# Rotation tables of a state-space layer: made later, on GpSimd, in the buffers where the scan reads them; weight chunks cut as halves; table work and loads in a new order

## The reference

```python
x = x + even_mixer(rms_norm(x, ...))          # RWKV-7 beside RG-LRU
x = x + conv_ffn(rms_norm(x, ...))            # first feed-forward
x = x + odd_mixer(rms_norm(x, ...))           # S5
x = x + conv_ffn(rms_norm(x, ...))            # second feed-forward
return rms_norm(x, final_norm_g)

def conv_ffn(xn, w_up, conv_w, conv_b, w_down):        # d_ff = 2816
    h = causal_dwconv(xn @ w_up, conv_w, conv_b)
    gate, val = split(h, 2)
    return (silu(gate) * val) @ w_down

def odd_mixer(xn, w_in, A_re, A_im, log_dt, B, C, D, w_glu):
    u = xn @ w_in                             # 64 groups of 16 channels, 64 complex states each
    ab = exp((A_re + i A_im) * dt); bb = (ab - 1) / A * B
    state[t] = ab * state[t-1] + bb @ u[t]    # associative scan over the sequence
    y = gelu(Re(C @ state) + D * u)
    val, gate = split(y @ w_glu, 2)
    return val * sigmoid(gate)
```

## Time and profile before

| | us |
|---|---|
| median of 3 runs (2630.66 to 2636.36) | 2632.98 |
| profiled execution, time | 2632.07 |
| its span | 2630.3 |

### The profile page before, as it was taken

The page is one execution under the profiler, slowest core; times in us unless marked ns, Lnnn a source line. Parts: engine busy times, 40 slices in busy tenths (PEclk is TensorE's granted clock), DMA queues, the critical chain, the costliest instruction groups (busy, mean ns, idle before and its releaser), DMA issues.

```text
span 2630.3 us, 33735 instructions
## 1 busy us (share of the span) xinstructions
PE 2481.5 (94%) x12861; PEld 2064.8 (78%) x12861; DVE 1473.8 (56%) x1902; ACT 1107.8 (42%) x1782; POOL 1320.7 (50%) x1120
## 2 busy tenths in 40 slices
PE   8999899999999999999888889999999999999997
PEld 6788788888777877887676668987878888888886
DVE  5442578786666676566656344663365656563223
ACT  5443345453445444453243334433254545452222
POOL 5322444453257767772577671112267777772221
PEclk9999999999999999999899889999999999999998
DMA  3111000000112222226344324651112222242312
GB/s 104 49 48 49 17 1 1 1 1 10 53 45 80 81 73 80 89 88 166 105 142 173 118 92 142 208 153 48 52 48 85 80 89 80 88 154 83 110 51 84
DMA packets 252963, 211.87 MB, mean 81 GB/s; under 512 B 25446, under 2 KB 228744, under 8 KB 250760
## 3 DMA queue, kind: packets, MB, share of 16 engines
q1 hardware_dynamic: 238599, 188.02, 22.8%
q10 hardware_dynamic: 14208, 21.76, 2.3%
HBM read 153.11 MB, written 52.43 MB: 78 GB/s over the span
## 4 chain that ended last, share of the span: by engine, by line
PE 59%; DVE 6%; POOL 5%; issue 2%; ACT 2%; DMA 0%; ACTq 0%; SPq 0%; DVEq 0%; POOLq 0%
PE acc_o L2172 14%; PE acc_o L1715 9%; PE bank_a L2172 8%; PE bank_a L2256 7%; PE bank_b L2256 7%; PE bank_b L2172 6%; PE acc_o L2713 2%; PE bank_a L3526 1%; POOL dense_lo L197 1%; PE bank_b L3549 1%; POOL t_gx L3051 1%; DVE x_late_l L2070 1%; POOL t_rot L3075 0%; DVE t_hx L3107 0%; POOL t_tmp L3075 0%
## 5 line engine op out<-in xcount | busy, mean ns | idle before, releaser
L197 POOL TENSOR_TENSOR dense_lo<-dense_raw,dense_hi 128x512 fp32r<-128x512 f32 (+3 forms) x142 | 178.2, 1256 | 494.4 <-ACT dense_hi L190 492.6
L190 ACT CAST dense_hi<-dense_raw 128x512 fp32r<-128x512 f32 (+3 forms) x142 | 79.4, 564 | 401.7 <-PE acc_o L1715 150.9
L2110 POOL TENSOR_TENSOR dense_lo<-w_raw_l,dense_hi 128x512 fp32r<-128x512 f32 x88 | 118.3, 1344 | 65.2 <-ACT dense_hi L2106 65.1
L2110 POOL TENSOR_TENSOR dense_lo<-w_sums_l,dense_hi 128x512 fp32r<-128x512 f32 x66 | 104.1, 1577 | 71.7 <-ACT dense_hi L2106 71.7
L2256 PE MATMUL bank_b<-h_hi_l,dense_hi 128*128 128x512 f32 x352 | 112.7, 402 | 26.0 <-POOL dense_lo L197 25.9
L403 PE MATMUL main_ps<-rounded 128*128 128x256 f32 x896 | 128.0, 294 | 8.9 <-DVE rounded L298 8.9
L197 POOL TENSOR_TENSOR w_lo_e<-w_raw_e,w_hi_e 128x512 fp32r<-128x512 f32 x42 | 56.3, 1344 | 158.0 <-ACT w_hi_e L190 158.0
L2110 POOL TENSOR_TENSOR w_l<-w_raw_l,w_l 128x512 fp32r<-128x512 f32 x88 | 115.0, 1306 | 40.9 <-ACT w_l L2106 40.9
L403 PEld LDWEIGHTS main_ps<-rounded 128*128 128x128 f32 x896 | 113.5, 190 | 27.3 <-DVE rounded L298 23.2
L2256 PE MATMUL bank_a<-h_hi_l,dense_hi 128*128 128x512 f32 x336 | 108.5, 405 | 23.7 <-POOL dense_lo L197 22.2
L2110 POOL TENSOR_TENSOR w_l<-w_sums_l,w_l 128x512 fp32r<-128x512 f32 x66 | 103.1, 1562 | 45.0 <-ACT w_l L2106 45.0
(11 more groups left out here) (544 smaller groups left out, 7085.7 us busy)
## 6 DMA issues: line engine op xcount, KB each, us to landing
w_raw_l<-in_f_w_up SPq DMA_DIRECT2D x176, 256.0 KB, 3.0
hidden<-val SPq DMA_DIRECT2D x44, 512.0 KB, 2.6
h_f_l<-hidden SPq DMA_DIRECT2D x44, 512.0 KB, 4.7
dense_raw<-in_f_w_down SPq DMA_DIRECT2D x72, 256.0 KB, 3.0
w_raw_e<-in_e_w_in SPq DMA_DIRECT2D x42, 256.0 KB, 2.9
s_states<-t_hx ACTq DMA_DIRECT2D x16, 512.0 KB, 2.9
s_inputs<-t_in ACTq DMA_DIRECT2D x16, 512.0 KB, 2.8
g_in<-s_inputs SPq DMA_DIRECT2D x8, 1024.0 KB, 5.2
```

The source lines that it names most:

```text
L190: nc.scalar.copy(self.hi[:, par, 0:n, :], self.raw[:, par, 0:n, :]).then_inc(w_hi_done, 1)
L197: pool.tensor_tensor(self.lo[:, par, 0:n, :], self.raw[:, par, 0:n, :], self.hi[:, par, 0:n, :].bitcast(F32), op=ALU.subtract).then_inc(w_ ...
L2110: pool.tensor_tensor(self.ring_lo[n % 4], self.source(ORDER[n % SEVEN]), self.ring_hi[n % 4].bitcast(F32), op=ALU.subtract).then_inc(q_lo, 1)
```

## The change

1. `chunks` cuts a unit in two nearly equal parts: 5 tiles as 3 and 2, 6 as 3 and 3; 7 and 8 stay 4 and 3, 4 and 4.
2. Rotation tables are made for four pairs at once, 8 times (`turns_pool(i, part)`), straight into `rot`, which has two buffers. Only table 0 is made in the first feed-forward (group 3, after the second chunk of units 2 and 3); table 1 at units 0 and 1 of the S5 product, tables 2 to 7 further on in it, each in two parts behind a chunk's subtraction. Table i waits for scan i-2. The stores and reads of `s5_turns` go, with their waits. `scan_dve` waits for POOL's count instead of a DMA.
3. A half on POOL is parted: products between the chunks, sums behind the second chunk.
4. `setup_dve(4)` moves to pair 11; steps 5, 6, 3 and 7 to units 1, 2, 3 and 7 of group 0; the transposes of C to units 3 and 5.
5. SP: B and C are loaded after the weights of unit 2 of group 0 instead of before them, hidden tiles of group 1 later; both first chunks of groups 1 to 3 ahead of the fetched tiles.
6. `first_act` makes `d_diag` first and stores the states last.

```diff
         def chunks(kt):
-            return [(k, min(KC, kt - k)) for k in range(0, kt, KC)]
+            n = (kt + 1) // 2
+            return [(0, n), (n, kt - n)]
...
             self.load_chunk(sp, 0, 1)
-            if self.tables:
-                self.tables.load_first_sp(sp, self.q_used0 + SEVEN * NP)
             for g in range(len(self.groups)):
                 fetched = list(self.next_tiles(g))
-                if g == 0:
-                    for m in fetched[:4]:
-                        self.fetch_sp(sp, m)
-                    self.hidden_sp(sp, NP - 1)
-                    fetched = fetched[4:]
-                else:
+                if g:
                     self.load_chunk(sp, g, 0)
-                    if self.tables:
-                        self.tables.beside_sp(sp, g, 1)
+                    self.load_chunk(sp, g, 1)
                     for m in fetched[:3]:
                         self.fetch_sp(sp, m)
-                    self.load_chunk(sp, g, 1)
                     fetched = fetched[3:]
                 for c in range(2, DT):
                     self.load_down(sp, g, c)
+                    if (g, c) == (0, 2):
+                        self.hidden_sp(sp, NP - 1)
+                        if self.tables:
+                            self.tables.load_first_sp(sp, self.q_used0 + SEVEN * NP)
                     for m in fetched[:2]:
                         self.fetch_sp(sp, m)
...
                     if self.tables:
-                        self.tables.beside_pool(pool, g, c)
+                        self.tables.beside_first_pool(pool, g, c)
                     if c > 1:
                         self.dn.take_lo(pool, n, self.down_unit(g) + c, 0, 1, 2)
+                    if self.tables:
+                        self.tables.beside_pool(pool, g, c, 2 * (self.down_unit(g) + c) + 4)
...
-    t_rot = [at(f"t_rot{s}", [P, 2, 2, N5], where) for s, where in enumerate((X_AT, Z_AT))]
+    rot = [at(f"rot{s}", [P, 4, 2, N5], where) for s, where in enumerate((Z_AT, Z_AT + 2 * TILE))]
+    t_tmp = at("t_tmp", [P, 2, 4, N5], X_AT + TILE)
...
             elif i in (8, 9, 10):
                 self.setup_dve(dve, i - 8)
+            elif i == 11:
+                self.setup_dve(dve, 4)
...
+        def beside_pool(self, pool, g, c, lo_done):
+            if self.half_of(g, c) is not None:
+                self.half_sums_pool(pool, self.half_of(g, c), lo_done)
+            elif g > self.HALF_GROUPS[-1] and c in (2, 3):
+                self.turns_pool(pool, 0, c - 2)
...
-        def turns_pool(self, pool, n):
-            pr = slice(2 * n, 2 * n + 2)
-            step = [P, 2, 8, 16]
+        def turns_pool(self, pool, i, part):
+            pr = slice(4 * i, 4 * i + 4)
+            step = [P, 4, 8, 16]
...
+            if part == 0:
+                if i == 0:
+                    pool.wait_ge(t_pe, 4 * HALVES)
+                    pool.wait_ge(t_kept, 11 * HALVES)
+                    pool.wait_ge(t_filters_out, 32 * HALVES)
+                elif i > 1:
+                    pool.wait_ge(s5_dve, 15 * (i - 1))
+                for o, a, b in ((turn[0], cos, far_cos), (tmp[0], sin, far_sin), (turn[1], sin, far_cos)):
+                    pool.tensor_tensor(o, a, b, op=ALU.mult).then_inc(t_turned, 1)
+            else:
+                pool.tensor_tensor(tmp[1], cos, far_sin, op=ALU.mult).then_inc(t_turned, 1)
+                pool.wait_ge(t_turned, 6 * i + 4)
+                pool.tensor_tensor(turn[0], turn[0], tmp[0], op=ALU.subtract).then_inc(t_turned, 1)
+                pool.tensor_tensor(turn[1], turn[1], tmp[1], op=ALU.add).then_inc(t_turned, 1)
...
-                read_turns(0)
                 load_unit(2)
                 read_filters(0)
                 read_states(0)
-                read_turns(1)
...
                 for n in range(DT):
-                    dn.take_lo(pool, DT, u_in + n, 0)
+                    for chunk in range(2):
+                        dn.take_lo(pool, DT, u_in + n, 0, chunk, chunk + 1)
+                        if n == 1:
+                            tables.turns_pool(pool, 1, chunk)
+                        elif n > 2:
+                            tables.turns_pool(pool, n - 1, chunk)
                 for n in range(len(PLACES)):
                     lo_place(pool, n)
+                    if n < 2:
+                        tables.turns_pool(pool, DT - 1, n)
...
-                    dve.wait_ge(rot_read[i % 2], 16 * (i // 2 + 1))
+                    dve.wait_ge(t_turned, 6 * i + 6)
```

More of the change, by code:

```diff
@@ L2216, in products_pe @@
                 down = self.down_unit(g)
-                for pair, k, n in self.pair_chunks(g):
+                for chunk, (pair, k, n) in enumerate(self.pair_chunks(g)):
                     for s in range(2):
@@ L2223, in products_pe @@
                             pe.wait_ge(f_lo, self.made + first + k + t + 2)
-                            last = self.down_tile(pe, g, s, k + t, self.down_place(g, k // KC, s), t)
+                            last = self.down_tile(pe, g, s, k + t, self.down_place(g, chunk, s), t)
                         last.then_inc(w_used, 1)
                     if self.tables:
-                        self.tables.beside_pe(pe, g, k // KC)
+                        self.tables.beside_pe(pe, g, chunk)
                 for c in range(2, DT):
@@ L2332, in load_sp @@
                     fetched = fetched[2:]
-                    if self.tables:
-                        self.tables.beside_sp(sp, g, c)
+                    if (g, c) == (0, 5) and self.tables:
+                        self.tables.load_second_sp(sp)
         def chunk_lo(self, pool, g, j):
@@ L3077, in turns_pool @@
[L3077 to L3084 removed]
+            if part == 0:
[12 more added lines that the diff above has]
+                pool.tensor_tensor(turn[1], turn[1], tmp[1], op=ALU.add).then_inc(t_turned, 1)
+                pool.wait_ge(t_turned, 6 * i + 6)
@@ L3138, in first_act @@
         def first_act(self, act, n):
-            self.keep_states(act, n)
+            for q in range(2):
+                nc.scalar.activation(d_diag[:, q, :], eye32[:, :], ACT.Copy,
+                                     scale=d_rows[:, 2 * n + q:2 * n + q + 1]).then_inc(t_kept, 1)
             act.wait_ge(t_pool, 8 * n + 8)
@@ L3143, in first_act @@
                                t_gx[:, part, :, 0, :].unsqueeze(2).to_broadcast([P, 2, 4, 32])).then_inc(t_kept, 1)
-            for q in range(2):
-                nc.scalar.activation(d_diag[:, q, :], eye32[:, :], ACT.Copy,
-                                     scale=d_rows[:, 2 * n + q:2 * n + q + 1]).then_inc(t_kept, 1)
+            self.keep_states(act, n)
         def half_act(self, act, n):
@@ L3186, in trunk @@
     fir = at("fir", [P, 4, 2, P], W_AT + 4 * TILE)
-    rot = at("rot", [P, 2, 4, 2, N5], W_AT + 5 * TILE)
     u_now = at("u_now", [P, 2, 4, 2, N5], B_AT)
@@ L3194, in trunk @@
     in_read, hx_read, fir_read = (sem(n + "_read") for n in ("in", "hx", "fir"))
-    rot_read = [sem(f"rot_read{s}") for s in range(2)]
     u_scaled = sem("u_scaled")
@@ L3396, in _ @@
                 ffn0.load_sp(sp)
-                for n in tables.TURNS[3, 7]:
-                    tables.keep_turns_sp(sp, n)
                 def load_unit(n):
@@ L3736, in up @@
                         ins.then_inc(s5_dve, 1)
-                    c_i, s_i = (rot[:, i % 2, :, k, :] for k in range(2))
+                    c_i, s_i = (rot[i % 2][:, :, k, :] for k in range(2))
                     up(nc.vector.tensor_copy(keep8[:, :, 1:N5], decay8[:, 4 * i:4 * i + 4].unsqueeze(2).to_broadcast([P, 4, N5 - 1])))
                     dve.wait_ge(s5_pe, inputs_done(i))
-                    dve.wait_ge(rot_read[i % 2], 16 * (i // 2 + 1))
+                    dve.wait_ge(t_turned, 6 * i + 6)
                     if i == DT - 1:
```

73 lines of the change are left out of this document (24 added, 49 removed).

## The result

The changed kernel takes 2570.69 us, the median of 4 runs (2568.31 to 2572.59), the kernel before 2632.36, also of 4. The ratio is 0.9763, its 95% interval 0.9746 to 0.978: 62 us faster. The forecast was 2564 us, the range 2546 to 2598. The profiled execution took 2569.76 us, its span is 2566.3, its mean clock 0.991.

What follows compares the result with a forecast made beforehand. PE, busy 94% of the span, was taken as the bound, its longest waits being for POOL's `dense_lo`. -66.5 - 2.4 - 1.5 + 1.2 = -69 from 2632.1 gave 2563, by the median 2564 us; range 2546 to 2598.

Steps and rivals of the forecast that it cites:

- The down part: First down product to first S5 product: 308 us instead of 374.5, 66 us less.
- Chunks of 3 and 2, sums behind: Down part: 2.7 us of PE work left after the first chunk's matmuls instead of 1.4; waits behind tables go.
- Group starts: Down part, two group starts: waits for the clearing of `t_fir` and ACT's copies, 4 us left, between 0 and 9.
- Loads in group 0: Unit 3's weights come late behind B and C in SP's queue: 5 us left, between 0 and 10.
- Table 0 in group 3: Its two parts on POOL barely fit before the next first chunk's subtraction: 2 us left, between 0 and 5.
- A unit with a half: Down part, groups 1 and 2: taken at 10.3 us each, 16 units, 164.8 us.
- The first rival's chain: A half's chain over POOL and ACT becomes the bound: 11.5 against 10.3 us a unit, 2583 us; chance 0.20.
- Setup step 4: Pair 11: seventeen small DVE instructions of 0.19 us each, some 4 us; 1.2 us lost, between 0 and 6.7.
- My last sign of being wrong: The prediction would be wrong if PE waits for DVE in pair 11.
- Tables 1 to 7: S5 stage: 8.4 us more POOL work a period costs nothing while it stays in the gap; periods still 20.7 us.
- The start: S5 stage's first chunk no longer waits behind two tables; 2.4 us of slow clock come back, between 0 and 2.4.
- The end: Last states wait less for `g_in` without reads of `rot`: 1.5 us come back, between 0 and 6.8.

Runs made afterwards that it cites:

- 3: The kernel before, with each rotation table made behind the second chunk of its unit instead of between the chunks: 2611.43 us, ratio 0.9917.
- 5: The changed kernel with POOL's sums of a half back between the two chunks, right behind the products: 2583.32 us, ratio 0.9803.
- 4: The kernel before with both the new cut of the chunks and the tables behind the second chunk: 2615.86 us, ratio 0.9941.
- 1: The kernel before with only the new cut of the chunks (3 and 2, 3 and 3): 2634.34 us, ratio 1.0006.
- 2: The changed kernel with the old cut of the chunks (4 and 1, 4 and 2): 2582.65 us, ratio 0.9809.
- 9: The changed kernel with the clearings of `t_hx` and `t_fir` moved from step 7 to unit 5 of group 0: 2566.21 us, ratio 0.974.
- experiment 8: The changed kernel with B and C loaded before the weights of unit 2 of group 0 again: 2563.89 us, ratio 0.9738.
- 10: The changed kernel with the three POOL products of the first part of tables 1 to 7 done twice: 2574.45 us, ratio 0.9782.
- 11: The changed kernel with the last read of `g_in` ahead of the first four y transfers in SP's queue: 2569.53 us, ratio 0.9766.
- 12: The changed kernel with B and C loaded before unit 2's weights, `t_hx` and `t_fir` cleared at unit 5, setup step 4 beside unit 0 of group 0: 2556.77 us.
- 6: The changed kernel with setup step 4 cut in four pieces, in pairs 11 to 14 of the up part: 2575.87 us, ratio 0.9791.

## Why the prediction was right, and where not

**The down part** was forecast at 308 us and took 310.70, so 63.8 instead of 66.5 us came back. That it was POOL's queue is shown by two moves within it: of the tables, 21 us (3), and of the sums, 12.6 us (5). That taking the tables out gave most of the rest is argued from 4 and 5.

- *Chunks of 3 and 2, sums behind.* The step was right as far as it went; 1, 2, 4 and 5 show that it holds for the two together only. Had the question been for the cut alone, my argument (2.7 us of cover instead of 1.4) would have been wrong by all it promised.
- *Group starts*, 4 us: 2.77 + 0.49 + 0.97 at the first, 0.49 + 0.96 at the second, 5.7 without the slow clock. The reason was the named one for most of the first: 9 removed 2.3 of the 2.77 and gave 4.5 us.
- *Loads in group 0*, 5 us: a wait of 4.68, and 6.8 us by the medians of experiment 8. That is 1.8 us over the forecast, as the group starts are 1.7 over theirs.
- *Table 0 in group 3*, 2 us: waits of 1.11 and 0.18.
- *A unit with a half*, 10.3 us: 10.20 in the mean of twelve. The first rival's chain (11.5) did not become the bound, though it is near: six waits for `t_gx`, five of them of 0.2 to 0.4 us.

**Setup step 4** is the term of the sum that was mis-sized: 1.2 us forecast, about 5 measured (4.8 by the matmuls of 1000 to 1060 us; the starts of the down part, which have more in them, have medians of 1203.3 us in seven kernels with it in pair 11, and 1196.9 in six without). I sized it by DVE's 0.19 us an instruction, though the row of 4.11 us for four such instructions in that same group already showed that 0.19 is the time with POOL idle. The failed sentence is "some 4 us", and with it the 1.2 us that I took from it; the bound of 6.7 held. My last sign of being wrong, PE waiting in pair 11, did come, by way of DVE, ACT and POOL. The Trainium skill (SBUF - State Buffer, "Reading the diagram") has that VectorE and GpSimd take their shared port pair for a whole instruction, whichever starts first, and that the other blocks meanwhile; for VectorE it names instructions with two SBUF inputs (against a GpSimd one that reads SBUF) or in a two-port mode. The trace agrees: three of the 17 instructions take 1.20 or 1.21 us instead of 0.18 to 0.19, and each ends 0.03 to 0.05 us after a POOL instruction of 1.29 us has ended. That is 3.1 us too much, against PE's wait of 3.08. No run has step 4 in pair 11 with POOL idle, so that the lock is the whole of the loss is argued from these sizes. I used it in the prediction against the long POOL work of the S5 stage only, where it cost PE nothing in the periods (10), and not where DVE's instructions are short and many.

**The S5 stage.** Tables 1 to 7 at nothing: right, a period is 20.73 us. Start and end were to give 2.4 + 1.5 = 3.9 us; the two profiles give 7.0.

- *The start*, 2.4 us: PE comes to the wait before the last states 161.0 us behind its first S5 product, in the kernel before, which waits 2.7 us for the first chunk, after 163.7. Experiments 3 and 4, which wait 8.5 and 8.8 us for that chunk, take 163.6 and 163.8; 1 and 2, with no wait and one of 1.0 us, take 161.1. So 2.7 us, by the step that I named.
- *The end*, 1.5 us: not borne out. The wait before the last states was to shrink because the reads of `rot` are gone. It is 3.23 us here instead of 4.36, but 3.13 to 5.13 in the eight profiles without these reads (10), and 3.70 to 4.66 in the four kernels that have them (before, 1, 3, 4). So no run shows this term. What holds the wait, by the one profile of 11, is the y transfers in front of `g_in` in SP's queue.
- *Luck*: behind the wait for `gate` the two profiles have the same waits, but 835.2 us are left here and 839.1 in the kernel before, which has 169 matmuls in the first 40 us where this one has 177. That is 4.0 of the 7.0 us, and all that differs is the granted clock (0.96 in the slower 40 us, 1.00 in the faster). From the first S5 product to the end the ten profiles of the changed kernel and its variants take 1051.1 to 1056.2 us with a median of 1055.2, against 1051.7 in this one. The kernel before takes 3.5 us more than that median.

The errors against the profiled execution's span: down part +2.7 us, its start +5.6 (6.8 for 1.2), behind it -3.1 (7.0 for 3.9, by luck), together 5.2. The medians are 6.7 above the forecast: this execution's time has 3.5 us around its span and that of the kernel before 1.8, which the prediction took over. The order inside `first_act` (part 6) was not tried by itself.

## What to carry to other kernels

When a queue serves two chunks in turn, write down for each chunk what stands before its subtraction and how much work of the consumer covers it. A new cut moves cover from one to the other, and here it was worth something only together with moving the work that stands there. A short instruction on DVE is to be priced by what POOL does at that moment, and a small serial block of them belongs in a stage where its engine is not on the way to the next product. What stands in a DMA queue ahead of the next weights, or at the end of a stage whose successor needs it, is late there. Two pieces of that sort and the small block, each put elsewhere, gave 14 us more together (12). A wait that one pair of profiles shows shorter need not be so: look at it in all runs that have the same work in front of it.

## What was not expected of the hardware

- DVE instructions of 128x32 take 0.19 us alone and 1.20 to 1.21 us beside a POOL that works without a gap, in pair 11 and again in pairs 12 to 14 (6). Instructions of 128x1024 beside it take 2.1 instead of 1.34 us (8.40 and 5.37 for four). But those of 128x512 that read a PSUM bank and `rot` take 0.68 us beside POOL's work as without it (10).
- POOL's product of 128x512 from `fine` and `coarse` takes 1.06 us, not twice the 0.62 of 128x256; beside DVE it takes 2.03.
- The same read of `g_in`, asked for at the same point of the S5 stage (156.2 to 156.4 us behind its first product), makes PE wait 3.13 us in one profile and 5.13 in another.
- With the same waits in that stretch, profiles differ by 4.7 us between 1725 and 2025 us through the granted clock alone (0.98 or 1.00 over 200 us). An effect of 4 us must be read from several runs, and then from the place of the edit.
